# Sums of squares of the heads in an encoder block: one fp32 product with ones becomes two products with rounded ones

## The chip, the cores and the metric

The kernel runs on one core of one Trainium2 chip. The metric is the time of one execution on the device, in microseconds (us); less is better. Engines: TensorE (PE, with its weight loads as PEld), VectorE (DVE), ScalarE (ACT), GpSimd (POOL) and SyncE (SP), which issues most transfers here.

## The reference

One encoder block for 512 tokens of width 2048, all in fp32. The part that the change touches is the normalization of each head of the first attention branch:

```python
def rmsnorm(x, g):
    x32 = x.astype(jnp.float32)
    y = x32 * lax.rsqrt(jnp.mean(x32 * x32, axis=-1, keepdims=True) + RMS_EPS)
    return (y * g.astype(jnp.float32)).astype(x.dtype)
...
        u = rmsnorm(h, g_mix[i])
        z = u @ w_in[i]
        qa, ka, va, cq, ckv, kr, ga, gb = jnp.split(z, SPLITS, axis=-1)

        qa = rmsnorm(qa.reshape(b, s, N_HEADS_A, HEAD_DIM_A), q_norm_a[i])
        ka = rmsnorm(ka.reshape(b, s, N_KV_A, HEAD_DIM_A), k_norm_a[i])
        qa = axial_rope(qa, ang_ra, ang_ca)
        ka = axial_rope(ka, ang_ra, ang_ca)
```

There are 8 query heads and 2 key heads of 128 dimensions, so ten sums of squares over 128 values for each of 512 tokens. Behind this stand attention, a second attention branch with low-rank latents, two gates, an output projection, a SwiGLU layer, a gated embedding and a last norm.

## The kernel before

**Layout.** Activations lie transposed: features on the 128 partitions, the 512 tokens along the free dimension. A sum over a head's features is then a sum over partitions, and is taken on PE: a product of a 128x128 matrix of ones with the squares gives the sum in every partition.

**Products.** Every large product is done in fp32r, a rounded fp32. Each operand is split into a rounded part (`hi`, written by ACT) and the rest (`lo`, written by DVE), and `product` (L310 to L312) sends three matmuls: hi·hi, hi·lo, lo·hi. Weights come in pieces of 4 x 128 rows by 256 columns into four buffers `raw`; ACT rounds a piece (`whi`, L678), DVE takes the rest (`wlo`, L1075), into two buffers each. So ACT may round piece n when PE has used piece n−2, and SP may load piece n+4 when DVE has split piece n.

**The start.** SP's queue issues, in this order: weight piece 0, `x` tiles 0 to 1 and 2 to 3, piece 1, `x` 4 to 7, piece 2, `x` 8 to 11, piece 3, `x` 12 to 15, the matrices `cm` (L214: identity, ones and two swaps, semaphore `mats_in`), and then piece 4, which waits for DVE's split of piece 0. ACT issues the gains. DVE sets `eps` (L1159), waits for the gains, and then does, for each four tiles of `x`, one `wlo` and four `gain_lo` (L1110), which give the low part of `u = x · gain`. PE's first group needs each tile of `u` in turn. The squares of `x` are taken by ACT between its other work (ten of the sixteen behind its rounding of piece 4) and added up by POOL; `first_total` on PE sums them with `ones` behind the sixth piece (L334). It is the first reader of the matrices.

**The heads.** The ten heads are numbered m = 0, 1 (keys) and 2 to 9 (queries). For each: ACT squares the head's tile into `res[:, 13]` (L711), PE's `head_total` (L338) multiplies it by the fp32 ones `cm[:, 1]` into bank 7, ACT takes logarithm and exponential of it, and DVE refines the root and scales the tile. The first three heads go beside the input groups 4, 5 and 6, the total standing behind a group's first piece. The other seven stand in the attention loop: head h's program, on every engine, prepares query head h+1. There PE does the scores, two weight pieces, `head_total`, two weight pieces, and so on; ACT does the four exponentials, the square, then `whi` of pieces b+2 and b+3; DVE does the softmax, then `wlo` of pieces b+2 and b+3. Each engine runs its program in the order written, and they are tied by semaphores alone.

Of the kernel before, what the change touches and what calls it, by code (L numbers as in the profile page):

```python
# [26 lines left out]
F32R = mybir.dt.float32r  # L27
ALU = mybir.AluOpType
# [3 lines left out]
P = 128  # L32
# [59 lines left out]
def build(nc, xT, pT, gains, tables, mats, w_in, w_qb, w_kvb, w_a, w_b, w_o, w_gu, w_dn, w_pg, w_pp, outT):  # L92
    with ExitStack() as ctx:
        def sb(name, shape, dt=F32):
            return ctx.enter_context(nc.sbuf_tensor(name, shape, dt))

        def sem(name):
            return ctx.enter_context(nc.semaphore(name))
# [4 lines left out]
        res = sb("res", [P, KD, SEQ])  # L103
# [7 lines left out]
        negmax = sb("negmax", [P, 4])  # L111
        psumrow = sb("psumrow", [P, 4])
        rrow = sb("rrow", [P, 4])

        r0 = sb("r0", [P, 8, 2, SEQ], F32R)
        r1 = sb("r1", [P, 8, 2, SEQ], F32R)
        r3 = sb("r3", [P, 8, 2, SEQ], F32R)
# [3 lines left out]
        ident, ones, swap_a, swap_b = (cm[:, i, :] for i in range(4))  # L121
        ps = ctx.enter_context(nc.psum_tensor("ps", [P, 8, SEQ], F32))
# [8 lines left out]
        gains_in, mats_in, tables_in, p_in = sem("gains_in"), sem("mats_in"), sem("tables_in"), sem("p_in")  # L131
# [3 lines left out]
        sq_done, acc_done, tot_done = sem("sq_done"), sem("acc_done"), sem("tot_done")  # L135
        log_done, root_done, refine, rstd_done = sem("log_done"), sem("root_done"), sem("refine"), sem("rstd_done")
        hsq, htot, hlog, hroot = sem("hsq"), sem("htot"), sem("hlog"), sem("hroot")
        hrefine, hnorm = sem("hrefine"), sem("hnorm")
        swapped, by_cos, by_sin, roped = sem("swapped"), sem("by_cos"), sem("by_sin"), sem("roped")
        v_turned, op_hi, op_lo = sem("v_turned"), sem("op_hi"), sem("op_lo")  # L140
# [26 lines left out]
        def ff_pair(g):  # L167
            return (g - G_FF + 2) % 4
# [8 lines left out]
        PT_B = [r1[:, 5], r1[:, 6], r1[:, 7]]  # L177
        PT_BANK = [4, 5, 7, 4]
        P_T = [r1[:, 4], r1[:, 5]]
        PROB = 8  # L180
        GATE_IN = [12, 8]

# [122 lines left out]
        def _(pe):  # L305
            mm = nc.tensor.matmul

            def product(out, hi, lo, x, start, stop):

                mm(out, hi, x[:, 0, :], start=start, stop=False)  # L310
                mm(out, hi, x[:, 1, :], start=False, stop=False)  # L311
                return mm(out, lo, x[:, 0, :], start=False, stop=stop)  # L312
# [21 lines left out]
                mm(ps[:, bank, :], ones, sums(norm), start=True, stop=True).then_inc(tot_done, 1)  # L334

            def head_total(m):
                pe.wait_ge(hsq, m + 1)
                mm(ps[:, 7:8, :], ones, res[:, 13:14, :], start=True, stop=True).then_inc(htot, 1)  # L338

            def head_swap(m, tile):  # L340
                pe.wait_ge(hnorm, m + 1)
# [26 lines left out]
            def turn_p(n, kt):  # L368
# [4 lines left out]
                for q in range(4):  # L373
                    i = nc.tensor.transpose(ps[:, PT_BANK[kt], q * P:(q + 1) * P],  # L374
                                            res[:, PROB + q, kt * P:(kt + 1) * P], ident)
                i.then_inc(p_turned, 1)
# [239 lines left out]
            for g in range(8):  # L616
# [4 lines left out]
                for t in range(2):  # L621
                    c = 256 * (g % 2) + P * t
                    for k in range(2):
                        i = product(ps[:, 2 * ff_pair(G_E + g) + t, :], hi[:, k, c:c + P], lo[:, k, c:c + P], P_T[k],
                                    k == 0, k == 1)
# [50 lines left out]
        def _(act):  # L676
            def copy(out, in_, scale=1.0):
                return nc.scalar.activation(out, in_, ACT.Copy, scale=scale)  # L678
# [30 lines left out]
            def head_square(m, tile, need, count):  # L709
                act.wait_ge(need, count)  # L710
                nc.scalar.activation(res[:, 13:14, :], tile, ACT.Square).then_inc(hsq, 1)  # L711

            def head_root(m):
                act.wait_ge(htot, m + 1)
                if not isinstance(m, int) or m > 0:
                    act.wait_ge(roped, m)
                nc.scalar.activation(res[:, 14, :], ps[:, 7, :], ACT.Ln, scale=1.0 / HD,
                                     bias=eps[:]).then_inc(hlog, 1)
                act.wait_ge(hlog, m + 1)
                nc.scalar.activation(res[:, 14, :], res[:, 14, :], ACT.Exp, scale=-0.5).then_inc(hroot, 1)  # L720
# [6 lines left out]
            def exps(n):  # L727
                for q in range(4):
                    act.wait_ge(max_done, n * 4 + q + 1)
                    if q == 0 and not (isinstance(n, int) and n == 0):  # L730
                        act.wait_ge(p_turned, n * 4)
                    nc.scalar.activation(res[:, PROB + q, :], ps[:, 4 + q, :], ACT.Exp, bias=negmax[:, q:q + 1],  # L732
                                         accum_out=psumrow[:, q:q + 1]).then_inc(exp_done, 1)
# [233 lines left out]
            for k in range(2):  # L967
                copy(P_T[k][:, 0, :], tab[:, 2 + k, :]).then_inc(u_hi, 1)

# [92 lines left out]
        def _(dve):  # L1062
            tt = nc.vector.tensor_tensor
# [3 lines left out]
            def wlo(n, j):  # L1067

                dve.wait_ge(w_hi_done, n + 1)
                if isinstance(n, int) and n >= LAST:  # L1070
                    dve.wait_ge(piece_used, N_D + 8)
                    tt(as_4_by_256(LAST_LO[:, j]), raw[:, j], as_4_by_256(LAST_HI[:, j]),
                       ALU.subtract).then_inc(w_lo_done, 1)
                    return
                tt(w_lo[:, j % HL], raw[:, j], w_hi[:, j % HL], ALU.subtract).then_inc(w_lo_done, 1)  # L1075
# [32 lines left out]
            def gain_lo(out, in_, gain, n):  # L1108
                dve.wait_ge(u_hi, n + 1)
                stt(out[:, 1, :], in_, gn[:, gain:gain + 1], out[:, 0, :], ALU.mult, ALU.subtract).then_inc(u_lo, 1)  # L1110

            def head_norm(m, tile, gain):

                refined(res[:, 14, :], res[:, 13, :], ps[:, 7, :], HD, hlog, hroot, m, hrefine, hrefine)
                dve.wait_ge(hrefine, m * 4 + 4)
                stt(tile, tile, gn[:, gain:gain + 1], res[:, 14:15, :], ALU.mult, ALU.mult).then_inc(hnorm, 1)
# [22 lines left out]
            def softmax(n):  # L1139
                for q in range(4):  # L1140
                    dve.wait_ge(scores, n * 4 + q + 1)
                    nc.vector.tensor_reduce(negmax[:, q:q + 1], ps[:, 4 + q, :], AX_X, ALU.max,  # L1142
                                            negate=True).then_inc(max_done, 1)
                for q in range(4):
                    dve.wait_ge(exp_done, n * 4 + q + 1)
                    nc.vector.reciprocal(rrow[:, q:q + 1], psumrow[:, q:q + 1]).then_inc(rsum_done, 1)
                    dve.wait_ge(rsum_done, n * 4 + q + 1)
                    nc.vector.tensor_scalar(res[:, PROB + q, :], res[:, PROB + q, :], rrow[:, q:q + 1], None,
                                            ALU.mult).then_inc(p_done, 1)
# [7 lines left out]
                tt(out[:, :, 1, :], ps[:, 6:7, :], out[:, :, 0, :], ALU.subtract).then_inc(o_lo, 1)  # L1157

            nc.vector.memset(eps[:], EPS).then_inc(set_done, 1)  # L1159
            dve.wait_ge(gains_in, 16)  # L1160
            for k in range(KD):
                if k % 4 == 0:
# [18 lines left out]
            dve.wait_ge(emptied, 4)  # L1181
            for m, (t, gain) in enumerate(((8, G_KN), (9, G_KN), (0, G_QN))):
                b = 16 + 4 * m
                wlo(b + 2, 2)
                head_norm(m, res[:, t:t + 1, :], gain)
                wlo(b + 3, 3)
                wlo(b + 4, 0)
                dve.wait_ge(hnorm, m + 1)
                rotate(m, res[:, t:t + 1, :], 0, res[:, 15:16, :], res[:, 14:15, :], P, 2 * m)
                dve.wait_ge(roped, m + 1)  # L1190
                op_split(2 * m, [K_A[0], K_A[1], Q_A][m], res[:, 15, :], SA if m == 2 else None)
                wlo(b + 5, 1)
                if m < 2:
                    op_split(2 * m + 1, V_A[m], ps[:, 4 + m, :])
                empty(res[:, 2 + 2 * m:4 + 2 * m, :], 2 * (m % 2), 0, b + 3)
# [6 lines left out]
            def gqa_head(h, kv, more):  # L1202
                b = h * 8 + N_GATE
                tile = res[:, bass.ds(h + 1, 1), :] if more else None
                softmax(h)
                wlo(b + 2, 2)
                wlo(b + 3, 3)
                if more:
                    head_norm(h + 3, tile, G_QN)
                wlo(b + 4, 0)  # L1210
                wlo(b + 5, 1)
                if more:
                    dve.wait_ge(hnorm, h + 4)
                    rotate(h + 3, tile, 0, res[:, 15:16, :], res[:, 14:15, :], P, h + 5)
                pt_split(h, 0, PT_A)
                pt_split(h, 1, PT_A)
                gate_group(h, 0, b + 3)
                if more:
                    dve.wait_ge(roped, h + 4)
                    op_split(h + 5, Q_A, res[:, 15, :], SA)  # L1220
                wlo(b + 6, 2)
                pt_split(h, 2, PT_A)
                pt_split(h, 3, PT_A)
                wlo(b + 7, 3)
                o_split(h, r3[:, bass.ds(h, 1)])
                wlo(b + 8, 0)
                wlo(b + 9, 1)
                gate_group(h, 1, b + 7)
# [161 lines left out]
            def chunk(c, last):  # L1390
                b, g = c * 24 + N_FF_LOOP, c * 12 + G_FF
                four(b)
                if isinstance(c, int) and c == 0:
                    dve.wait_ge(p_in, 16)
                    for k in range(2):
                        dve.wait_ge(u_hi, 41 + k)
                        tt(P_T[k][:, 1, :], tab[:, 2 + k, :], P_T[k][:, 0, :], ALU.subtract).then_inc(u_lo, 1)
                else:
# [211 lines left out]
```

## Time and profile before

| | |
|---|---|
| median of 3 runs | 2858.02 us (2857.79 to 2858.09) |
| the profiled execution | 2858.06 us, span 2856.3 us |
| mean granted TensorE clock | 0.997 |
| PE busy | 2820.7 us, 99% of the span |
| DVE busy | 1211.7 us, 42% |
| ACT busy | 857.1 us, 30% |
| POOL busy | 235.0 us, 8% |
| moved | 286.94 MB, mean 100 GB/s |

Busy time is the union of an engine's instructions as the profiler recorded them. Matmuls overlap in the pipeline, so the time that one costs in a row of them is the distance between two starts, and not its own duration. Positions are microseconds from the start of the span.

### The profile page before, as it was taken

The numbers are of one execution on the slowest core, as the hardware profiler recorded it, in microseconds if no ns is written. First come the engines' busy times: TensorE is split into PE (matmuls) and PEld (weight loads), VectorE is DVE, ScalarE is ACT, GpSimd is POOL, SyncE is SP. The second block draws the span as 40 slices with busy tenths as digits, with TensorE's granted clock in tenths as the row PEclk, the third lists the DMA queues.
The fourth block names the chain that finished last, engine by engine and source line by source line (L and its number), as shares of the span: only waits on it lengthen the run. The fifth ranks groups of instructions, "written<-read, shape, count | busy, mean of one in ns | idle before, by whom it ended". The sixth has DMA issues, their size and how long they took to land.

```text
span 2856.3 us, 32227 instructions
## 1 busy us (share of the span) xinstructions
PE 2820.7 (99%) x12562; PEld 2321.1 (81%) x12562; DVE 1211.7 (42%) x1267; ACT 857.1 (30%) x1053; POOL 235.0 (8%) x134
## 2 busy tenths in 40 slices
PE   8999999999999999999999999999999999999998
PEld 6888888887778888888888888888888888888787
DVE  5445545436763334333333333333343333335535
ACT  5234434323442223222222222222222222224433
POOL 3000000000001101100000000000000000004342
PEclk9999999999999999999999999999999999999999
DMA  6333333331124442333333333333323333233232
GB/s 202 91 90 103 101 96 103 103 104 59 44 67 133 156 154 94 110 97 96 96 95 95 95 96 98 99 96 95 95 95 95 96 98 99 96 95 96 89 96 96
DMA packets 274543, 286.94 MB, mean 100 GB/s; under 512 B 8752, under 2 KB 260656, under 8 KB 274352
## 3 DMA queue, kind: packets, MB, share of 16 engines
q1 hardware_dynamic: 269984, 277.64, 31.2%
q10 hardware_dynamic: 4496, 8.44, 0.8%
q8 instruction: 42, 0.69, 0.1%
q14 instruction: 21, 0.17, 0.0%
HBM read 273.46 MB, written 12.58 MB: 100 GB/s over the span
## 4 chain that ended last, share of the span: by engine, by line
PE 72%; DVE 2%; ACT 1%; POOL 1%; issue 1%; DVEq 0%; ACTq 0%; POOLq 0%
PE ps L310 24%; PE ps L312 24%; PE ps L311 24%; POOL tab L1511 1%; DVE w_lo L1075 0%; DVE r L1110 0%; PE ps L374 0%; ACT r L678 0%; DVE res L1087 0%; ACT tab L696 0%; DVE emb L1478 0%; ACT w_hi L678 0%; POOL acc L1511 0%; DVE res L1371 0%; PE ps L347 0%
## 5 line engine op out<-in xcount | busy, mean ns | idle before, releaser
L310 PE MATMUL ps<-r,w_hi 128*128 128x512 f32 x3840 | 1505.8, 392 | 12.7 <-DVE r L1110 8.2
L312 PE MATMUL ps<-r,w_lo 128*128 128x512 f32 x3840 | 1495.4, 389 | 0.0
L311 PE MATMUL ps<-r,w_hi 128*128 128x512 f32 x3840 | 1495.3, 389 | 0.0
L1075 DVE TENSOR_TENSOR w_lo<-raw,w_hi 128x1024 fp32r<-128x1024 f32 x484 | 612.9, 1267 | 1494.5 <-ACT w_hi L678 1493.3
L678 ACT ACTIVATE w_hi<-raw 128x1024 fp32r<-128x1024 f32 x484 | 512.7, 1060 | 1642.9 <-PE ps L312 1634.4
L310 PEld LDWEIGHTS ps<-r,w_hi 128*128 128x128 f32 x3840 | 721.6, 188 | 171.6 <-issue 13.8
L311 PEld LDWEIGHTS ps<-r,w_hi 128*128 128x128 f32 x3840 | 721.7, 188 | 152.6 <-issue 4.3
L312 PEld LDWEIGHTS ps<-r,w_lo 128*128 128x128 f32 x3840 | 721.5, 188 | 150.4
L1527 POOL TENSOR_TENSOR tmp<-tmp 128x1024 f32<-128x1024 f32 x22 | 52.6, 2391 | 1339.0 <-DVE tmp L1087 1339.0
L1371 DVE TENSOR_TENSOR res<-ps,res 128x1024 f32<-128x1024 f32 x96 | 116.8, 1217 | 0.0
L1087 DVE TENSOR_TENSOR tmp<-ps,rstd 128x1024 f32<-128x1024 f32 x71 | 86.4, 1218 | 1.6 <-PE ps L312 1.5
L310 PE MATMUL ps<-r 128*128 128x512 f32 (+2 forms) x224 | 84.3, 376 | 1.1 <-DVE r L1133 0.8
L312 PE MATMUL ps<-r 128*128 128x512 f32 (+2 forms) x224 | 81.5, 364 | 0.0
L311 PE MATMUL ps<-r 128*128 128x512 f32 (+2 forms) x224 | 81.4, 363 | 0.0
L1511 POOL TENSOR_TENSOR acc<-acc,tab 128x512 f32<-128x512 f32 x43 | 66.2, 1540 | 157.3 <-ACT tab L696 153.7
L678 ACT ACTIVATE r<-ps 128x512 fp32r<-128x512 f32 (+1 forms) x90 | 50.4, 594 | 64.6 <-PE ps L374 34.7
L1110 DVE SCALAR_TENSOR_TENSOR r<-res,gn,r 128x512 fp32r<-128x512 f32 x48 | 46.9, 1011 | 22.3 <-ACT r L678 22.3
L1508 POOL COPY acc<-tmp 128x512 f32<-128x512 f32 x3 | 2.1, 704 | 607.6 <-ACT tmp L696 576.6
L310 PEld LDWEIGHTS ps<-r 128*128 128x128 f32 (+1 forms) x224 | 42.8, 191 | 11.0 <-issue 2.1
L732 ACT ACTIVATE res<-ps,negmax 128x512 f32<-128x512 f32 x64 | 43.4, 688 | 19.8 <-DVE negmax L1142 19.7
L312 PEld LDWEIGHTS ps<-r 128*128 128x128 f32 (+1 forms) x224 | 42.8, 191 | 6.9
L311 PEld LDWEIGHTS ps<-r 128*128 128x128 f32 (+1 forms) x224 | 43.0, 192 | 5.5
(98 smaller groups left out, 900.8 us busy)
## 6 DMA issues: line engine op xcount, KB each, us to landing
raw<-w_gu SPq DMA_DIRECT2D x176, 512.0 KB, 3.6
raw<-w_in SPq DMA_DIRECT2D x108, 512.0 KB, 3.7
raw<-w_dn SPq DMA_DIRECT2D x88, 512.0 KB, 3.4
raw<-w_o SPq DMA_DIRECT2D x32, 512.0 KB, 3.4
raw<-w_pg SPq DMA_DIRECT2D x32, 512.0 KB, 3.4
gates<-tmp ACTq DMA_DIRECT2D x16, 512.0 KB, 2.9
raw<-w_a SPq DMA_DIRECT2D x16, 512.0 KB, 3.4
raw<-w_b SPq DMA_DIRECT2D x16, 512.0 KB, 3.4
```

The lines of the kernel that those rows point to most:

```text
L310: mm(out, hi, x[:, 0, :], start=start, stop=False)
L311: mm(out, hi, x[:, 1, :], start=False, stop=False)
L312: return mm(out, lo, x[:, 0, :], start=False, stop=stop)
L678: return nc.scalar.activation(out, in_, ACT.Copy, scale=scale)
L732: nc.scalar.activation(res[:, PROB + q, :], ps[:, 4 + q, :], ACT.Exp, bias=negmax[:, q:q + 1], accum_out=psumrow[:, q:q + 1]).then_inc(exp ...
L1075: tt(w_lo[:, j % HL], raw[:, j], w_hi[:, j % HL], ALU.subtract).then_inc(w_lo_done, 1)
L1087: tt(out, ps[:, bank:bank + 2, :], both(r), ALU.mult).then_inc(emptied, 1)
L1110: stt(out[:, 1, :], in_, gn[:, gain:gain + 1], out[:, 0, :], ALU.mult, ALU.subtract).then_inc(u_lo, 1)
L1371: tt(r, ps[:, 2 * pair:2 * pair + 2, :], r, ALU.add).then_inc(emptied, 1)
L1508: nc.gpsimd.tensor_copy(out, sq[:, s % 2, :]).then_inc(acc_done, 1)
L1511: nc.gpsimd.tensor_tensor(out, out, sq[:, s % 2, :], ALU.add).then_inc(acc_done, 1)
L1527: nc.gpsimd.tensor_tensor(tmp[:, 2:4, :], tmp[:, 2:4, :], tmp[:, 0:2, :], ALU.mult).then_inc(ff_mul, 1)
```

## The change

The squares of a head are split as the operands of the other products are: ACT rounds them into `SQ_PARTS[:, 0]`, DVE writes the rest into `SQ_PARTS[:, 1]`, and PE sums each part with an fp32r copy of the ones. `SQ_PARTS` lies in a slot of `r3` that nothing else uses at the time. DVE makes the fp32r ones at the start of its program, when the matrices have landed.

```diff
+        ones_r = sb("ones_r", [P, P], F32R)
...
+        hsq_hi, hsq_lo, ones_set = sem("hsq_hi"), sem("hsq_lo"), sem("ones_set")
...
+        SQ_PARTS = r3[:, 7]
...
             def head_total(m):
-                pe.wait_ge(hsq, m + 1)
-                mm(ps[:, 7:8, :], ones, res[:, 13:14, :], start=True, stop=True).then_inc(htot, 1)
+                if isinstance(m, int) and m == 0:
+                    pe.wait_ge(ones_set, 1)
+                pe.wait_ge(hsq_lo, m + 1)
+                mm(ps[:, 7, :], ones_r[:], SQ_PARTS[:, 0, :], start=True, stop=False)
+                mm(ps[:, 7, :], ones_r[:], SQ_PARTS[:, 1, :], start=False, stop=True).then_inc(htot, 1)
...
             def head_square(m, tile, need, count):
                 act.wait_ge(need, count)
                 nc.scalar.activation(res[:, 13:14, :], tile, ACT.Square).then_inc(hsq, 1)
+                act.wait_ge(hsq, m + 1)
+                copy(SQ_PARTS[:, 0:1, :], res[:, 13:14, :]).then_inc(hsq_hi, 1)
...
+            def head_square_lo(m):
+                dve.wait_ge(hsq_hi, m + 1)
+                tt(SQ_PARTS[:, 1, :], res[:, 13, :], SQ_PARTS[:, 0, :], ALU.subtract).then_inc(hsq_lo, 1)
...
             nc.vector.memset(eps[:], EPS).then_inc(set_done, 1)
+            dve.wait_ge(mats_in, 16)
+            nc.vector.tensor_copy(ones_r[:], ones).then_inc(ones_set, 1)
             dve.wait_ge(gains_in, 16)
...
             for m, (t, gain) in enumerate(((8, G_KN), (9, G_KN), (0, G_QN))):
                 b = 16 + 4 * m
+                head_square_lo(m)
                 wlo(b + 2, 2)
...
                 softmax(h)
+                if more:
+                    head_square_lo(h + 3)
                 wlo(b + 2, 2)
```

## Rows read from the trace of the kernel before

**Rows 1.** The page, busy time of each engine, share of the span, instructions.
```profile
PE 2820.7 (99%) x12562; PEld 2321.1 (81%) x12562; DVE 1211.7 (42%) x1267; ACT 857.1 (30%) x1053; POOL 235.0 (8%) x134
```

**Rows 2.** The page, the chain that ended last, by engine.
```profile
PE 72%; DVE 2%; ACT 1%; POOL 1%; issue 1%; DVEq 0%; ACTq 0%; POOLq 0%
```

**Rows 3.** Timeline of DVE at the start: start us, duration us, instruction.
```profile
6.19 1.22 DVE L1075 TENSOR_TENSOR w_lo<-raw,w_hi 128x1024 fp32r<-128x1024 f32 x1 [5.31 <-ACT w_hi L678]
7.33 2.73 DVE L1110 SCALAR_TENSOR_TENSOR r<-res,gn,r 128x512 fp32r<-128x512 f32 x4
```

**Rows 4.** Timeline of PE at the start; in brackets the idle time before, and its releaser.
```profile
8.22 0.76 PE L310 MATMUL ps<-r,w_hi 128*128 128x512 f32 x1 [8.22 <-DVE r L1110]
8.78 0.63 PE L311 MATMUL ps<-r,w_hi 128*128 128x512 f32 x1
9.21 0.63 PE L312 MATMUL ps<-r,w_lo 128*128 128x512 f32 x1
...
13.82 0.39 PE L311 MATMUL ps<-r,w_hi 128*128 128x512 f32 x1
...
45.74 1.10 PE L334 MATMUL ps<-acc,cm 128*128 128x512 f32 x2 [2.04 <-POOL acc L1511]
```

**Rows 5.** Groups by line: busy us, mean ns; idle before them, what ended it.
```profile
L678 ACT ACTIVATE w_hi<-raw 128x1024 fp32r<-128x1024 f32 x484 | 512.7, 1060 | 1642.9 <-PE ps L312 1634.4 <-ACT tmp L806 4.6 <-DMA raw<-w_in 2.7
```

**Rows 6.** Timeline of PE about the first head total.
```profile
94.70 0.39 PE L310 MATMUL ps<-r,w_hi 128*128 128x512 f32 x1
...
96.06 1.02 PE L338 MATMUL ps<-res,cm 128*128 128x512 f32 x2
...
99.46 0.39 PE L312 MATMUL ps<-r,w_lo 128*128 128x512 f32 x1
```

**Rows 7.** The same view, four groups near in kind to what is added.
```profile
L1133 DVE TENSOR_TENSOR r<-res,r 128x512 fp32r<-128x512 f32 x11 | 8.6, 784 | 2.3 <-ACT r L678 2.3
L678 ACT ACTIVATE r<-res 128x512 fp32r<-128x512 f32 x31 | 19.5, 630 | 34.7 <-DVE res L1128 27.4 <-DVE res L1087 7.2
L1146 DVE RECIPROCAL rrow<-psumrow 128x1 f32<-128x1 f32 x64 | 10.1, 158 | 11.5 <-ACT res L732 11.5
L1148 DVE TENSOR_SCALAR res<-res,rrow 128x512 f32<-128x512 f32 x64 | 31.2, 487 | 2.3
```

**Rows 8.** Timeline of ACT before the total at 280.96 us.
```profile
277.14 0.64 ACT L711 ACTIVATE res<-res 128x512 f32 x1
277.66 1.07 ACT L678 ACTIVATE w_hi<-raw 128x1024 fp32r<-128x1024 f32 x1
```

**Rows 9.** Timeline of PE there.
```profile
280.96 1.02 PE L338 MATMUL ps<-res,cm 128*128 128x512 f32 x2
```

**Rows 10.** Timeline of DVE before the second head's total.
```profile
117.29 1.21 DVE L1087 TENSOR_TENSOR res<-ps,rstd 128x1024 f32<-128x1024 f32 x1
```

**Rows 11.** Timeline of PE at that total.
```profile
120.13 1.02 PE L338 MATMUL ps<-res,cm 128*128 128x512 f32 x2
```

**Rows 12.** Timeline of DVE before 280.96 us, the split of a weight piece.
```profile
278.76 1.23 DVE L1075 TENSOR_TENSOR w_lo<-raw,w_hi 128x1024 fp32r<-128x1024 f32 x1 [0.78 <-ACT w_hi L678]
```

**Rows 13.** Timeline of SP's queue at the start: start us, us that issuing took.
```profile
8.06 1.25 SPq L213 DMA_DIRECT2D res<-xT  x1
9.35 3.35 SPq L214 DMA_DIRECT2D cm<-mats  x1
```

**Rows 14.** Transfers issued about 9 us: size of one, us from issue to landing.
```profile
res<-xT SPq DMA_DIRECT2D x1, 1024.0 KB, 12.3
cm<-mats SPq DMA_DIRECT2D x1, 256.0 KB, 11.7
```

**Rows 15.** Stretches of 5 us: busy us (instructions) of PE, PEld, DVE, ACT, POOL, granted clock, DMA share, GB/s.
```profile
685.00:690.00 5.00, 3.69 (x11) 2.88 (x12) 3.36 (x6) 1.68 (x4) 0.00 (x0) 0.61 0.00 0
690.00:695.00 5.00, 5.00 (x16) 3.52 (x16) 3.57 (x6) 1.65 (x4) 0.00 (x0) 0.71 0.28 93
```

**Rows 16.** Timeline of PE ahead of that.
```profile
685.51 0.66 PE L347 MATMUL ps<-cm,res 128*128 128x128 f32 x4 [1.95 <-DVE res L1087]
```

## The prediction

> **What bounds the kernel now.** I read the page first. TensorE (PE) is busy for 2820.7 us of a span of 2856.3 us [rows 1], so the kernel is one long row of matmuls, and there are two ways only in which an edit can move its time: it changes how long PE's own row takes, or it makes PE stand still. The chain that ended last says the same: PE holds 72% of it, and no other engine more than 2% [rows 2]. Work on VectorE (DVE) and ScalarE (ACT) costs nothing as long as PE doesn't come to wait for it. So I then read, in the timelines, the two stretches that the diff touches: the start, and the places where a head's sum of squares is taken.
>
> At the start PE stands still until 8.22 us. It is released by the first gained and split tile of `u`, which DVE writes at 7.33 us, right behind its first split of a weight piece at 6.19 us [rows 3, 4]. From there on PE runs without a gap until 43.7 us, where it stands for 2.04 us, until GpSimd (POOL) has added the last square of `x` [rows 4]. In the whole trace ACT waits only 2.7 us for weight pieces from memory, and 1634 us for PE to free their buffers [rows 5]: what keeps the start moving is PE's own pace, and not the transfers.
>
> At a head total, PE sends the fp32 product as two instructions (the x2 in [rows 6]), so 20 for the ten heads.
>
> **The change part by part.**
>
> *1. The product (removed and added, on PE's row).* From the matmul at 94.70 to the head total at 96.06 there are 6 matmuls, 0.227 us each [rows 6]. From the head total's start at 96.06 to the matmul at 99.46 there are the two fp32 instructions and 11 matmuls of the plain kind [rows 6]: 3.40 − 11 × 0.227 = 0.91 us for the two, 0.45 us each. The new form is two fp32r matmuls, 128x128 by 128x512, which is exactly the kind that takes 0.227 us beside it: 2 × 0.227 = 0.45 us. The saving is 0.91 − 0.45 = 0.45 us a head and 10 × 0.45 = 4.5 us in all. Bounds: an fp32r product that costs what an fp32 instruction does saves nothing; no row shows a 512-column matmul under 0.227 us, so no more than 4.5 us. I take 4.5, since the added instructions have the same type and shape as their neighbours.
>
> *2. The hidden steps before it (added, on ACT and DVE).* Each head gains a rounding copy on ACT (nearest row: the copy of a head's tile, 0.63 us) and a subtraction on DVE (nearest row: 0.78 us) [rows 7], ten of each, 14 us of work. PE now waits for the subtraction and not for the square. In the loop I take the head total at 280.96 us, whose square ends latest before it: the square runs from 277.14 for 0.64 us and ends at 277.78 [rows 8]; copy until 278.4; subtraction until 279.2; DVE has nothing to do in the 0.78 us before its w_lo at 278.76 [rows 12], so it is free to begin. That leaves 1.7 us before PE comes for it [rows 9]. For the second key head DVE is busy until 117.29 + 1.21 = 118.50 [rows 10], the subtraction ends at 119.3, and PE comes at 120.13 [rows 11]: 0.8 us are left. Cost on the path: none.
>
> What is queued behind them matters more: the split of weight piece b+2. ACT's w_hi at 277.66 [rows 8] and DVE's w_lo at 278.76 both go back by about 0.65 us, so w_lo ends at about 279.4 + 1.23 = 280.6. PE wants it right after the new head total, at 280.96 + 0.45 = 281.4. 0.8 us are left of 1.9. Again nothing, but if that cover were gone, 14 us of copies and subtractions would come onto PE's row.
>
> *3. The wait at the start (added, at the head of DVE's queue).* This is the part that decides. `ones_r` is filled by DVE, and the wait for `mats_in` that this needs stands in front of DVE's first wait for the gains, so in front of everything DVE does. The matrices are the tenth transfer of SP's queue. Their issue begins at 9.35 us [rows 13] and they land 11.7 us later [rows 14], at 21.05 us. Queued ahead of them are the whole of `x` and the four first weight pieces. Queued behind the wait on DVE: the first w_lo, then all sixteen `gain_lo`. PE waits for both; ACT's third w_hi waits for PE's first piece; POOL's squares wait for ACT; SP's fifth weight load waits for DVE's first w_lo, so it goes out after 22 us, in place of right behind the matrices, which hurts no one, since its buffer is read at PE's pace.
>
> DVE's first w_lo moves from 6.19 us to 21.05 plus the copy of `ones`. For that copy, 128 columns wide, the nearest rows are 0.16 us (one column) and 0.49 us (512 columns) [rows 7]; I take 0.25. 21.05 + 0.25 − 6.19 = 15.1 us. PE starts at 8.22 + 15.1 = 23.3 us. Does any of it come back? It would have to come out of a stall that isn't itself behind PE. The 2.04 us at 43.7 us is behind PE: the last ten squares of `x` stand on ACT behind w_hi 4, which waits for PE's third piece. So they move along, and the stall stays. Until the end PE has no other wait of any size for memory [rows 5]. The whole 15.1 us goes to the end. Bounds: 15.0 with the copy at 0.16, 15.3 with 0.49.
>
> *4. PE's clock.* In its first stretch PE runs at 0.43 us a matmul, from 8.78 to 9.21 and so on, and at 0.227 us only from about 13.8 us [rows 4]: that is the level of 1.2 GHz, before 2.4 GHz. The 5.6 us at half speed cost 2.8 us. I let that stretch move along unchanged, at no cost. If it came out half as long or half as long again, the sum would move by 1.4 us either way.
>
> The Trainium skill ("TensorE: Matmul & The Clock Gate", Part 1) says that the clock is held at half until PE has been active, and that the monitor behind it runs freely and isn't reset when a kernel starts. By the trace alone the slow stretch travels with PE's start; by the page it may come out shorter or longer for a start that is 15 us later, with the sum lower or higher by up to the 1.4 us worked out above.
>
> **Sum.** +15.1 − 4.5 = +10.6 us. The profiled execution took 2858.06 us, 1.8 us more than its span; it stands within 0.04 us of the median of the three timed runs, 2858.02. So 2858.0 + 10.6 = 2868.6 us, 0.37% slower. About 0.2%, 5.7 us, is what a measurement of this kernel can tell from no change.
>
> **The rivals.**
>
> *The matrices land early, and the wait is short (not slower).* All of part 3 hangs on the landing at 21.05 us. The price is one for one: each microsecond earlier is one off the sum. Under 16.1 us the sum is within 0.2%, and at 6 us, where DVE starts today, the wait is free and 2858.0 − 4.5 = 2853.5 us is left, 0.16% faster. For it: the transfer is small, 256 KB. Against it: the one before it on the queue was issued at 8.06 [rows 13] and landed 12.3 us later [rows 14], at 20.4, so the matrices come 0.7 us behind it, in their turn; nothing in the change issues them sooner. Chance 3%.
>
> *The product saves nothing.* If the two rounded products cost what the two fp32 instructions cost, the change doesn't do on PE what it says, and only part 3 is left: 2858.0 + 15.1 = 2873.2 us. For it: no row shows a sum over `ones` in fp32r. Against it: 3840 neighbours of the same type and shape. Chance 5%.
>
> *The clock falls elsewhere.* Once in this trace, between 685 and 695 us, the granted clock falls, to a mean of 0.61 and 0.71 in two stretches of 5 us [rows 15]. (0.39 + 0.29) × 5 × 2 = 6.8 us were spent at the lower level, and cost half of that, 3.4 us. Ahead of it PE had waited 1.95 us for DVE [rows 16]. If the move makes that fall vanish, the time is 2865.2 us; if another one comes, the stall of 2.04 us at the start being the likeliest place, 2872.0 us. For it: that stall is as long as the one ahead of the fall, and no row tells why one had a fall behind it and the other not. Against it: the four executions before differ by 0.3 us only, so whatever sets the fall repeats. Chance 14%, both signs together. The free-running monitor of the page named above speaks for this rival.
>
> *The subtraction is late.* If PE waits for DVE at every head, the copy and the subtraction, 0.63 + 0.78 = 1.4 us, come onto PE's row ten times: 2882.7 us. The smallest cover is 0.8 us, so the work on DVE would have to be late by more than one of its own instructions. Chance 3%.
>
> **How the numbers follow.** The forecast holds 75%: 2868.6 us, its own range 2867 to 2870 by the copy of `ones` and the slow stretch. The range reaches to the vanished fall of the clock below, 2865, and to the product that saves nothing above, 2873.2; left out are the late subtraction and the early landing, 6%, and what I haven't thought of. Slower by over 0.2%: 96%. Within 0.2%: 3%, part of the early landing and some loss I overlooked that comes back. Faster by over 0.2%: 1%, since even a free wait gives only 0.16%.
>
> **What would show it.** In the profile after: DVE's first w_lo at about 21.3 us in place of 6.19, and PE's first matmul at about 23.3, released by the first `gain_lo`; the stall before the first total still near 2 us; fifth weight load issued after 22 us; each head total two instructions 0.227 us apart, with the next matmul 0.45 us behind its start; no new wait of PE for the subtraction; ten more copies of 0.6 us on ACT and ten subtractions of 0.7 to 0.8 us on DVE. The prediction is wrong if PE starts before 20 us, if a later gap of PE shrinks by what the start lost, or if the granted clock falls in other places than before.

## The result, and the profile after

The changed kernel takes 2867.51 us (median of 7 runs, 2866.75 to 2868.01) against 2857.81 us before (7 runs, 2857.73 to 2858.33): a ratio of 1.0034, 95% interval 1.0025 to 1.0044. It is 9.7 us slower. The profiled execution took 2867.43 us, with a span of 2865.6 us.

The page of the changed kernel, busy time of each engine; PE has 5.5 us less than in [rows 1], in a span that is 9.3 us longer:

```profile
PE 2815.2 (98%) x12562; PEld 2320.5 (81%) x12562; DVE 1219.1 (43%) x1278; ACT 863.6 (30%) x1063; POOL 234.8 (8%) x134
```

**The start.** Timelines of DVE, of PE and of SP's queue in the changed kernel, and its transfers issued about 9 us (size, us to landing). They answer to [rows 3], [rows 4], [rows 13] and [rows 14]:

```profile
20.90 0.23 DVE L1173 CAST ones_r<-cm 128x128 fp32r<-128x128 f32 x1 [20.02 <-DMA cm<-mats]
21.05 1.22 DVE L1083 TENSOR_TENSOR w_lo<-raw,w_hi 128x1024 fp32r<-128x1024 f32 x1
22.18 2.73 DVE L1118 SCALAR_TENSOR_TENSOR r<-res,gn,r 128x512 fp32r<-128x512 f32 x4
```

```profile
23.07 0.77 PE L313 MATMUL ps<-r,w_hi 128*128 128x512 f32 x1 [23.07 <-DVE r L1118]
23.64 0.63 PE L314 MATMUL ps<-r,w_hi 128*128 128x512 f32 x1
...
26.08 0.40 PE L314 MATMUL ps<-r,w_hi 128*128 128x512 f32 x1
...
59.36 1.37 PE L337 MATMUL ps<-acc,cm 128*128 128x512 f32 x2 [2.06 <-POOL acc L1528]
```

```profile
9.24 3.35 SPq L217 DMA_DIRECT2D cm<-mats  x1
22.29 16.56 SPq L205 DMA_DIRECT2D raw<-w_in  x4
```

```profile
cm<-mats SPq DMA_DIRECT2D x1, 256.0 KB, 11.6
```

DVE stands for 20.02 us until the matrices land (9.24 + 11.6 = 20.84 us), copies the ones in 0.23 us and does its first split at 21.05 us, where it did it at 6.19. PE starts at 23.07 us instead of 8.22, 14.85 us later. SP's fifth weight load goes out at 22.29 us and hurts no one: in all of the trace ACT waits 2.6 us for pieces of `w_in`, where it waited 2.7 before ([rows 5]). The stall ahead of the first total is there as before, 2.06 us for 2.04.

**The heads.** PE at the first head total; it answers to [rows 6]:

```profile
110.83 0.39 PE L315 MATMUL ps<-r,w_lo 128*128 128x512 f32 x1
111.05 0.39 PE L343 MATMUL ps<-r,ones_r 128*128 128x512 f32 x1
111.28 0.39 PE L344 MATMUL ps<-r,ones_r 128*128 128x512 f32 x1
111.51 0.39 PE L313 MATMUL ps<-r,w_hi 128*128 128x512 f32 x1
```

The two rounded products lie in the row like any others, 0.23 us apart. The ten totals start from 111.05 to 501.98 us; before it was from 96.06 to 491.07. The tenth total, before and then after:

```profile
491.07 1.02 PE L338 MATMUL ps<-res,cm 128*128 128x512 f32 x2
```

```profile
501.98 0.39 PE L343 MATMUL ps<-r,ones_r 128*128 128x512 f32 x1
```

That is 390.93 us for 395.01, 4.08 us less over nine totals: 0.453 us each, 4.5 us for ten. The other traces agree: all four with the fp32 product (the kernel before twice, runs 2 and 9 below) have 395.01 us between these two totals, and those of the changed kernel and of runs 1, 3, 5, 7 and 8 have 390.92 or 390.93, whatever the clock did ahead of them.

DVE, then PE, at the total whose cover was worked out ahead of the run; they answer to [rows 12] and [rows 9]:

```profile
291.20 0.69 DVE L1122 TENSOR_TENSOR r<-res,r 128x512 fp32r<-128x512 f32 x1 [0.50 <-ACT r L684]
292.15 1.23 DVE L1083 TENSOR_TENSOR w_lo<-raw,w_hi 128x1024 fp32r<-128x1024 f32 x1 [0.26 <-ACT w_hi L684]
```

```profile
293.69 0.39 PE L343 MATMUL ps<-r,ones_r 128*128 128x512 f32 x1
293.91 0.39 PE L344 MATMUL ps<-r,ones_r 128*128 128x512 f32 x1
294.14 0.39 PE L313 MATMUL ps<-r,w_hi 128*128 128x512 f32 x1
```

The subtraction ends at 291.89, 1.8 us before PE comes; the split of the weight piece ends at 293.38, 0.76 us before PE needs it at 294.14. PE waits for neither. The largest waits of PE in the changed kernel (who waited for what, us in total, times, longest) are those of the kernel before, with the first grown from 8.2 us:

```profile
PE ps L313 <- DVE r L1118: 23.1, 1, 23.1
PE ps L313 <- DVE w_lo L1083: 4.5, 5, 1.1
PE ps L380 <- DVE r L1165: 3.0, 5, 0.6
```

**The clock.** Stretches of the changed kernel, with the columns of [rows 15]; the granted clock is the third number from the end. In the first one it fell where it hadn't fallen before (in both traces the records of it below full clock are at one half, the lower level of 1.2 GHz):

```profile
57.00:66.00 9.00, 6.95 (x22) 4.86 (x21) 7.35 (x7) 3.32 (x5) 2.08 (x2) 0.81 0.38 117
690.00:700.00 10.00, 7.11 (x26) 5.03 (x27) 8.30 (x12) 3.06 (x6) 0.00 (x0) 0.92 0.09 26
700.00:710.00 10.00, 10.00 (x40) 7.55 (x39) 9.04 (x17) 5.89 (x13) 0.00 (x0) 0.91 0.16 52
```

**Where the time went.** The same instruction of PE in both traces gives the lag of the changed kernel along its way. The last landmarks are the four transposes behind the stall of 1.96 us in the second branch ([rows 16]) and those behind the next small one. Before, then after:

```profile
705.93 0.66 PE L374 MATMUL ps<-cm,res 128*128 128x128 f32 x4 [0.60 <-DVE r L1153]
```

```profile
695.98 0.66 PE L353 MATMUL ps<-cm,res 128*128 128x128 f32 x4 [1.96 <-DVE res L1095]
...
715.28 0.66 PE L380 MATMUL ps<-cm,res 128*128 128x128 f32 x4 [0.60 <-DVE r L1165]
```

| landmark of PE | before | after | lag | since the last |
|---|---|---|---|---|
| first matmul | 8.22 | 23.07 | +14.85 | the wait for the matrices |
| first total | 45.74 | 59.36 | +13.62 | −1.23, slow stretch at the start is shorter |
| first head total | 96.06 | 111.05 | +14.99 | +1.37, the clock falls at 60 us |
| last head total | 491.07 | 501.98 | +10.91 | −4.08, nine totals |
| stall in the second branch | 685.51 | 695.98 | +10.47 | −0.44, the tenth |
| behind it | 705.93 | 715.28 | +9.35 | −1.12, the fall there is shorter |
| span | 2856.3 | 2865.6 | +9.3 | nothing |

The wait gives +14.85, the products −4.5, the clock −1.0: +9.35 us, which is the difference of the two profiled executions (9.37) and 0.3 us under that of the medians (9.7). In both traces the clock is also at half in the last 9.5 to 10 us. That costs nothing: PE has no work left there, and from its last stall (2.16 us) to the end both kernels take 12.63 us. The kernel before:

```profile
2847.00:2856.00 9.00, 0.00 (x0) 0.00 (x0) 4.43 (x4) 0.00 (x0) 0.00 (x0) 0.50 0.69 234
```

### The profile page after: what moved, and what is told of

The parts are those of the page before. It is cut to its first block, busy times and chain, and to the rows that moved or that the text cites. A ratio compares the mean times of both kernels' runs of the same rounds, so it can differ in the third digit from the quotient of the medians.

```text
span 2865.6 us, 32249 instructions
## 1 busy us (share of the span) xinstructions
PE 2815.2 (98%) x12562; PEld 2320.5 (81%) x12562; DVE 1219.1 (43%) x1278; ACT 863.6 (30%) x1063; POOL 234.8 (8%) x134
## 4 chain that ended last, share of the span: by engine, by line
PE 71%; DVE 2%; ACT 1%; POOL 1%; issue 1%; DVEq 0%; ACTq 0%; POOLq 0%
PE ps L313 24%; PE ps L315 24%; PE ps L314 24%; POOL tab L1528 1%; DVE w_lo L1083 0%; DVE r L1118 0%; PE ps L380 0%; ACT r L684 0%; ACT tab L702 0%; DVE res L1095 0%; DVE emb L1495 0%; ACT w_hi L684 0%; POOL acc L1528 0%; DVE res L1388 0%; PE ps L353 0%
```

## The experiments

"Run 1" and so on are the numbers of these experiments. All times are medians; "before" is the kernel before, run on the same chip among them: 2857.54 us for the first four, 2857.80 us for the next four, 2857.86 us for the last three.

**1. The wait further down.** Does the place of the wait make the loss?

```diff
-            dve.wait_ge(mats_in, 16)
-            nc.vector.tensor_copy(ones_r[:], ones).then_inc(ones_set, 1)
             dve.wait_ge(gains_in, 16)
...
             for n in range(4, 8):
                 wlo(n, n % 4)
+            dve.wait_ge(mats_in, 16)
+            nc.vector.tensor_copy(ones_r[:], ones).then_inc(ones_set, 1)
             recip(0, 0, 7, 0, D)
```

> The changed kernel with one edit: DVE's wait for the matrices and its copy of the ones stand behind its eighth split of a weight piece and no longer ahead of its whole program. My theory, that the place of the wait is the whole loss: PE starts at 8.2 us again, DVE never waits for the matrices (they land at 21 us, DVE comes for them at about 47 us), and the ten products give 4.5 us: 2857.8 - 4.5 = 2853.3 us, down to 2851.5 if the fall of the granted clock at about 685 us comes out shorter, as it did in the changed kernel. Rival, that the added copies and subtractions cost something by themselves: 2855 us or more, with PE waiting at the head totals.

Measured: 2852.55 us (2851.50 to 2853.08, 11 runs), ratio to before 0.9983 (0.9974 to 0.9992). The same two instructions, 15 us less than the changed kernel, and 5.0 us less than the kernel before. DVE's timeline:

```profile
6.10 1.22 DVE L1083 TENSOR_TENSOR w_lo<-raw,w_hi 128x1024 fp32r<-128x1024 f32 x1 [5.22 <-ACT w_hi L684]
...
46.80 0.21 DVE L1180 CAST ones_r<-cm 128x128 fp32r<-128x128 f32 x1
```

DVE begins at 6.10 us, and comes for the matrices at 46.8 us, with no wait. The loss is the place of the wait, and the rival (the added copies and subtractions cost something) falls: the products bring what they should, with all of their preparation in place.

**2. The wait alone.** The other half: the kernel before, with `ones_r`, the wait and the copy added at the head of DVE's program as in the change, and nothing that reads it.

> The kernel before with one edit: DVE waits for the matrices and copies the ones at the head of its program; nothing reads the copy, the products stay fp32. My theory: PE's start moves from 8.2 to 23.1 us as in the changed kernel, 14.85 us; the slow stretch at the start comes out 1.2 us cheaper and a new fall of the clock behind the first total costs 1.4 us, as in the changed kernel: about 2872.7 us, within 1.5 us for the fall at 685 us. It should lie 4 to 5 us above the changed kernel. Rival, that the products bring nothing and the loss at the start is smaller than it looks: as the changed kernel, 2867.5 us.

Measured: 2872.62 us (2872.29 to 2873.65, 5 runs), ratio 1.0056 (1.0042 to 1.0069; the two medians give 1.0053). +15.1 us for the wait alone; with −5.0 us for the rest alone (run 1) that makes +10.1, against the +9.7 of the whole change. The two halves add up within what the clock moves. PE's first matmul:

```profile
23.27 0.77 PE L312 MATMUL ps<-r,w_hi 128*128 128x512 f32 x1 [23.27 <-DVE r L1112]
```

**3. The ones from POOL.** No wait and no copy on DVE at all:

```diff
-            dve.wait_ge(mats_in, 16)
-            nc.vector.tensor_copy(ones_r[:], ones).then_inc(ones_set, 1)
...
         def _(pool):
+            nc.gpsimd.memset(ones_r[:].bitcast(F32), 1.0).then_inc(ones_set, 1)
```

> The changed kernel with one edit: the rounded ones are written by a memset on POOL, which is idle at the start, and DVE's wait for the matrices and its copy are gone. My theory: the same time as with the wait further down, 2853.3 us (2851.5 to 2853.5), since both take all of the wait off PE. Rival, that DVE's copy or its wait costs something even where PE doesn't see it: this one is faster than that by 0.2 us or more.

Measured: 2852.22 us (2851.34 to 2853.08, 11 runs), ratio 0.9983 (0.9974 to 0.9992): not to be told from run 1, whose runs spread over 1.6 us. The memset takes 0.20 us at 0.74 us on POOL. A wait that no one sees costs nothing, so this version has no advantage but that it can't be put in the wrong place.

**4. One product instead of two.** Run 1, with the product of the low part left out (the sum is then that of the rounded squares).

> The kernel with the wait further down, and with one of the two products of a head total left out: the sum is taken of the rounded part of the squares alone, so the low part is missing from it. It prices one added product: by my theory 0.227 us a head, 2.3 us for ten: 2851.0 us, and the next matmul of PE starts 0.23 us behind the head total. Rival, that a rounded product costs something else than its neighbours in the row: another difference than 2.3 us, 0 if the stop behind it and not its length sets the pace.

Measured: 2851.36 us (2850.03 to 2851.84, 11 runs), 1.2 us less than run 1 and not 2.3. The trace says 0.227 all the same:

```profile
96.05 0.39 PE L315 MATMUL ps<-r,w_lo 128*128 128x512 f32 x1
96.27 0.39 PE L343 MATMUL ps<-r,ones_r 128*128 128x512 f32 x1
96.50 0.39 PE L313 MATMUL ps<-r,w_hi 128*128 128x512 f32 x1
```

From the first to the last head total it takes 388.89 us (96.27 to 485.16) where run 1 takes 390.93 (96.67 to 487.60): 2.04 us over nine, 0.227 each. The price is the row's. Why the medians differ by less isn't shown; they hold the clock as well, which moves between executions of one kernel by about as much (runs 10 and 11), and the intervals of the two ratios overlap (0.9970 to 0.9988 here). A difference of 1 us between medians of this kernel doesn't price an instruction.

**5. One more subtraction a head, and 6. three more.** How much cover lies behind the added work? On run 1 (the sixth kernel has `range(3)` and `m * 3 + i`, so three further subtractions one after the other; `junk` is a scratch tile and `extra` a semaphore):

```diff
             def head_square_lo(m):
                 dve.wait_ge(hsq_hi, m + 1)
+                for i in range(1):
+                    if not isinstance(m, int) or m or i:
+                        dve.wait_ge(extra, m * 1 + i)
+                    tt(junk[:], res[:, 13, :], SQ_PARTS[:, 0, :], ALU.subtract).then_inc(extra, 1)
                 tt(SQ_PARTS[:, 1, :], res[:, 13, :], SQ_PARTS[:, 0, :], ALU.subtract).then_inc(hsq_lo, 1)
```

> The kernel with the wait further down (2852.6 us), with one more subtraction of the same shape on DVE ahead of each head's own, into a scratch tile. My theory, that 0.8 to 1.0 us of cover lie behind the subtraction (the trace of that kernel has 0.94, 1.03 and 1.00 us at the first three heads and 0.76 to 0.9 us behind the split of a weight piece in the loop): the 0.73 us stay hidden, 2852.6 us, within 0.7. Rival, that the cover is already used up: about 0.7 us a head, 2859 us.

> As the kernel before, with three more subtractions a head in place of one, 2.2 us. My theory: the cover is passed. 1.2 us at each of the first three heads (PE waits for the subtraction), nothing at the fourth, 0.7 at the fifth and 1.1 at each of the last five (PE waits for the split of a weight piece): 9.8 us, 2862.4 us. Rival, that DVE's work in the loop has far more room than I read, since it is idle for half of it: 3.6 us of the first three heads at most, 2856 us.

Measured: 2852.17 us (2851.67 to 2853.14, 11 runs) with one, no more than run 1. With three 2863.22 us (2861.30 to 2863.97, 11 runs), ratio to before 1.0019 (1.0010 to 1.0028), and 10.7 us more than run 1 where I had worked out 9.8. Waits of PE with three:

```profile
PE ps L315 <- DVE w_lo L1085: 6.9, 11, 1.1
PE ps L345 <- DVE r L1128: 3.6, 5, 1.1
```

The second row is the wait that the prediction's last rival spoke of, PE for the subtraction: about 1.05 us at each of the first three heads. The first row has grown from 4.5 to 6.9 us: PE waits for the split of the weight piece queued behind the subtractions. The last five heads of the loop take 53.1 to 53.3 us each instead of 52.1. These idle times are less than what is lost, since the idle time before a matmul counts only from the end of the last one's 0.39 us, and matmuls that don't wait start 0.227 us apart. The landmarks hold the whole: against run 5, whose trace had no fall of the clock there either, it is 1.20 us more from the first total to the first head total, 8.34 from there to the tenth and 0.82 from there to the stall in the second branch, 10.4 us. So the cover is real and small: it takes one instruction more of this kind, and three turn the gain into a loss. Two weren't run.

**7. The first total later.** On run 3, `in_group(1, {2: [first_total]})` in place of `{1: [first_total]}`.

> The kernel whose ones come from POOL (2852.2 us), with the first total one weight piece later on PE, so that POOL's last square is there when PE comes. It is for the clock. Theory A, that the fall of the clock at 45 to 60 us in four of the six traces comes of PE's stall of 2 us ahead of it: stall and fall go together; 2.0 us of stall are gone and in most executions 1.4 us of slow clock, against up to 1.1 us of a new wait for the split of the ninth piece, since DVE empties the first group later: 2850.0 us, with no fall between 40 and 65 us. Theory B, that the fall has nothing to do with the stall: it stays, and 2851.3 us.

Measured: 2855.96 us (2855.06 to 2856.38, 11 runs), 3.7 us more than run 3. Neither theory was tested, since the stall did not go away; it only changed its name. PE, then ACT, in that kernel:

```profile
46.54 0.50 PE L313 MATMUL ps<-r,w_hi 128*128 128x512 f32 x1 [3.04 <-DVE w_lo L1083]
...
60.99 0.47 PE L313 MATMUL ps<-r,w_hi 128*128 128x512 f32 x1 [0.75 <-DVE w_lo L1083]
```

```profile
42.66 0.63 ACT L702 ACTIVATE tmp<-res 128x512 f32<-128x512 f32 x1 [0.80 <-POOL acc L1526]
43.20 1.99 ACT L684 ACTIVATE w_hi<-raw 128x1024 fp32r<-128x1024 f32 x2
```

ACT rounds the seventh weight piece only behind the last square, at 43.2 us, and its squares wait for POOL. DVE's split comes behind that, and PE stands for 3.04 us. In the other kernels the first total fills part of that time. The two waits shown are 3.79 us, where run 3's trace has 2.08 us ahead of its total; and the clock rose 5.3 us behind PE's first matmul, in run 3's trace 3.5, which is 0.9 us more at half speed. Together that is 2.6 of the 2.8 us by which the two spans differ; what the medians differ by beyond that isn't traced. Taking one release away shows the next one, right behind it.

**8. The matrices first.** The changed kernel, whose wait stays at the head of DVE's program, with the transfer moved to the front of SP's queue:

```diff
             x_v = xT.rearrange("(k p) s -> p k s", p=P)
+            sp.dma_start(cm[:], mats).then_inc(mats_in, 16)
             load(0, 0, w_in, 0, C_K)
...
             sp.dma_start(res[:, 12:16, :], x_v[:, 12:16, :]).then_inc(x_in[3], 16)
-            sp.dma_start(cm[:], mats).then_inc(mats_in, 16)
```

> The changed kernel with one edit: SP issues the matrices first and no longer tenth; DVE's wait for them stays at the head of its program. My theory, that the loss is the landing at 21 us and not the wait as such: the matrices land before 5 us, the wait is over when DVE has its first work, and what is left is their 0.5 us of issuing ahead of the first weights and of x: PE starts at 8.7 us, 2853.1 us. Rival, that DVE held up at the head of its program costs as much wherever the matrices stand: near 2867.5 us.

Measured: 2853.57 us (2852.90 to 2853.88, 11 runs), ratio 0.9985 (0.9976 to 0.9994). The transfer, DVE, and PE:

```profile
cm<-mats SPq DMA_DIRECT2D x1, 256.0 KB, 3.0
```

```profile
3.73 0.23 DVE L1173 CAST ones_r<-cm 128x128 fp32r<-128x128 f32 x1 [2.85 <-DMA cm<-mats]
```

```profile
9.43 0.77 PE L313 MATMUL ps<-r,w_hi 128*128 128x512 f32 x1 [9.43 <-DVE r L1118]
```

The wait is where it was and costs nothing, because it ends at 3.7 us, ahead of DVE's first work. What is left is that all other loads come behind the matrices: ACT begins to round the first tiles of `u`, for which it waits for `x`, at 7.78 us instead of 6.45, and PE starts 1.2 us later than before (I had 0.5). The landing is what counts, as the first rival said; its condition just isn't met in the change.

**9. A late start without a transfer.** On the kernel before:

```diff
                 if k % 4 == 0:
                     wlo(k // 4, k // 4)
+                if k == 0:
+                    nc.vector.memset(emb[:, 0:4, :], 0.0)
                 gain_lo(u_tile(k), res[:, k, :], G_MIX + k, k)
```

> The kernel before with one instruction more: DVE writes zeros to 2048 elements a partition of a tile that is free then, behind its first split of a weight piece and ahead of the first gain_lo. It holds up PE's start by some 2 us (a split of 1024 elements takes 1.22 us, 2048 elements between 1.1 and 2.4 us) with no wait for a transfer in it. My theory, that a late start of PE goes to the end one for one: the time is longer by what PE's first matmul is later, 1 to 2.4 us, within 0.7 us for the clock. Rival, that a small delay is taken up by the stall of 2.0 us ahead of the first total or by waits behind it: 2857.6 us, no change.

Measured: 2859.64 us (2859.13 to 2860.32, 11 runs) against 2857.86 (15 runs): +1.8 us. DVE and PE:

```profile
7.71 1.76 DVE L1165 MEMSET emb<- 128x2048 f32 x1 [0.38 <-issue]
```

```profile
10.17 0.76 PE L310 MATMUL ps<-r,w_hi 128*128 128x512 f32 x1 [10.17 <-DVE r L1110]
```

PE starts 1.95 us later and the end comes 1.8 us later. By its ratio (1.0006, 0.9997 to 1.0015) this run alone does not exclude no change. Run 2 (15.05 us later at the start, 15.1 at the end) does: there a late start is paid in full, and this run agrees with that.

**10. The kernel before again, and 11. the changed kernel again,** one execution each, for a second trace.

> The kernel before, unchanged, for a second trace of it. Its first trace had PE's clock rise at 13.7 us, no fall behind the first total, and 6.8 us at the lower level from 686 us. If the places of the rise and the falls differ from one execution to another, this trace has others with the same instructions, and its time differs by what they cost, up to 3 us. If they belong to the kernel, it has the same three figures within 0.3 us.

> The changed kernel, unchanged, for a second trace of it. Its first trace had PE's clock rise at 25.9 us, a fall of 3.4 us at 60 us and one of 3.4 us at 698 us. If these differ from one execution to another, this trace has other ones. Apart from the clock it must have PE's first matmul at 23.1 us within 0.4.

Measured: 2857.31 and 2867.11 us, 9.8 us apart. The stretch from 40 to 50 us in the first trace of the kernel before and then in its second:

```profile
40.00:50.00 10.00, 7.96 (x33) 5.72 (x32) 5.37 (x6) 5.09 (x7) 5.13 (x4) 1.00 0.25 73
```

```profile
40.00:50.00 10.00, 7.79 (x26) 5.49 (x25) 6.21 (x7) 4.48 (x6) 4.21 (x4) 0.83 0.30 92
```

The instructions are the same; in the second one the clock fell. It also rose earlier at the start (11.3 us for 13.7), and the fall behind the stall in the second branch lasted 3.4 us and not 6.8. The changed kernel's second trace had its rise at 28.2 us for 25.9, and no fall near 60 us. PE's first matmul is at 8.19 and 23.02 us, 0.03 and 0.05 us from the first traces. So when the clock rises, whether it falls at the first total, and how long it falls in the second branch belong to the execution, and the start to the kernel.

## Why the prediction was right

**The sum.** Forecast 2868.6 us, +10.6; measured 2867.5 us, +9.7. It lies in the range of 2865 to 2873.2, and in the narrower one of 2867 to 2870. (The upper end is 0.1 us off its own sum: 2858.0 + 15.1 is 2873.1.) Of the signs of being wrong that the prediction named, one came true: the granted clock fell in another place than before, at 60 us. The other two did not: PE started at 23.07 us, and no later gap of PE shrank by what the start had lost.

**Part 1, the product:** forecast 0.45 us a head; 0.453 in the traces. Right, and the rival that the product saves nothing is out, by runs 1 and 4.

**Part 2, the hidden steps:** forecast 1.7 and 0.8 us of cover in the loop, and 0.8 at the second key head; 1.8, 0.76 and 1.02 in the trace. The nearest row for the subtraction, 0.78 us, was a little high: it takes 0.69. Runs 5 and 6 show that the cover is there and ends where the traces put it. The rival of the late subtraction holds with three further subtractions, and not with one.

**Part 3, the wait at the start:** forecast a first split at 21.3 us, PE at 23.3, 15.1 us; measured 21.05, 23.07 and 14.85. The matrices landed 0.2 us sooner. Runs 1, 2, 3 and 8 take the wait away, have it alone, replace it, and let it end early; each goes as this part says. That nothing of the delay comes back was argued from the order of ACT's work; the table of landmarks and run 2 show it for 15 us, and run 9, within its noise, for 2 us. The reason given for the stall at 43.7 us was incomplete: run 7 shows that the split of the seventh piece would hold PE there, had POOL's squares not done so.

**Part 4, the clock:** this is the term that was mis-sized. "I let that stretch move along unchanged, at no cost": it got 1.23 us cheaper, a fall at 60 us cost 1.37 us, and the fall in the second branch got 1.12 us cheaper, −1.0 us in all. That this came to −1.0 and not to +1.0 was luck, as runs 10 and 11 show: the same kernels had rise and falls otherwise in their second traces. The rule of the Trainium skill ("TensorE: Matmul & The Clock Gate", Part 1), that the monitor runs freely and isn't reset by a kernel's start, agrees with these traces (rise at 13.7 and 11.3 us for the same first matmul at 8.2 us). Over all 13 traces the rise came 2.85 to 5.98 us behind PE's first matmul. "Once in this trace" was not right either: the clock also fell at 2846.8 us, at no cost, as shown above. What I held against the rival that the clock falls elsewhere was wrong: "the four executions before differ by 0.3 us only, so whatever sets the fall repeats". Among 27 later runs of the kernel before were times from 2854.61 to 2858.66 us. Its price was wrong too: I gave the fall of 6.8 us in the second branch half its length, 3.4 us. From the stall there to the next landmark the kernel before takes 705.93 − 685.51 = 20.42 us, the changed kernel, with a fall half as long, 19.30, and run 1, with none, 18.24. So the fall cost 2.2 us, and one half as long costs 0.8 to 1.1 us in the eleven traces that have it. PE stood idle in part of it: [rows 15] show 3.69 us busy of the first 5, of which the stall took 0.5.

**The rival on the other side,** the early landing: refused by the change's own trace (20.84 us) and confirmed as a mechanism by run 8.

## What to carry to other kernels

A wait is charged to everything queued behind it on its engine: before putting a one-off preparation at the head of a program, look up when its operand lands (issue time plus landing time) and put it behind the last work that doesn't need it. Here the same two instructions cost 15 us at one place and nothing at another, three times what the whole idea brings. And where PE is busy for 99%, price an edit by the distance of two landmarks in the traces with no fall of the clock between them: it gave 0.453 and 0.227 us, where the medians of runs 1 and 4 were 1 us off.

## What was not expected of the hardware

- In the 13 traces of this kernel's versions the clock fell behind the second branch's stall of 1.96 us in 12 (for 3.4 us; 6.8 us in one), and behind the stall at the first total in 7, run 7's behind the stall that took its place. The stalls that had a fall behind them at that place were of 1.9 to 2.2 and 3.0 us, and those that had none of 1.8 to 2.1 us. The first trace of the kernel before and the later one differ in this with the same instructions. What decides it within an execution stays open: run 7 was meant to take the stall away and didn't.
- A transfer of 256 KB took 3.0 us from issue to landing at the head of the queue and 11.7 us as the tenth on it, behind the 4.2 MB of `x` and the 2.1 MB of four weight pieces. Here the landing time was set by what stood ahead in the queue, and not by the transfer's size.
